# RWKV chunk pipeline: chunks seven phases apart instead of six, state-space groups every three steps instead of two

## The chip, the cores and the metric

The program runs on one core of one Trainium2 chip. The metric is the device time in microseconds (us) of one execution of the whole program. The core has a matrix engine (TensorE, PE in the rows; PEld is its weight load), a vector engine (VectorE, DVE), a scalar engine (ScalarE, ACT), GpSimd (POOL) and SyncE (SP), which only issues transfers here. Each engine works through its own list of instructions in order, and they wait for each other by semaphores.

## What is computed

Two layers of a decoder for a prompt of 2048 tokens and eight sample tokens. Layer 0 has an RWKV-7 recurrence and an S5 state-space layer side by side; the change touches only how these two are interleaved.

```
def step(s, inp):                      # RWKV-7, 8 heads of 64, for each token
    r_t, w_t, k_t, v_t, a_t, b_t = inp
    sa = jnp.einsum('bhvk,bhk->bhv', s, a_t)
    s = s * w_t[:, :, None, :] + sa[..., None] * b_t[:, :, None, :] + v_t[..., None] * k_t[:, :, None, :]
    return s, jnp.einsum('bhvk,bhk->bhv', s, r_t)
...
cr, ci, sr, si = lax.associative_scan(_cplx_combine, (a_re, a_im, bu_re, bu_im), axis=1)   # S5, 32 groups
h_re = sr + cr * h0r - ci * h0i
h_im = si + cr * h0i + ci * h0r
y = jnp.einsum('btgp,gcp->btgc', h_re, c_re) - jnp.einsum('btgp,gcp->btgc', h_im, c_im)
y = jax.nn.gelu(y)
```

## The kernel before

The program is a row of stages: projections of layer 0, the stage `rc` (function `rwkv_chunks`), the samples of layer 0, its output projection, then layer 1. Stages do not overlap: each ends with a barrier of all engines.

**RWKV.** In `rc` the 2048 tokens are 32 chunks of 64. The work of a chunk is 16 **phases** (`PHASES`), numbered 0 to 15 here. In each phase PE multiplies something into the chunk's own PSUM tile `bk` and then one other engine carries it to SBUF, for the next phase to read:

- phase 0 (`M_`): PE lines 1648 and 1651; DVE lines 1807, 1809, 1813. POOL then makes the masked tiles `ct` (line 1847)
- phase 1 (`KV`): PE 1660, 1664; ACT line 1763 (1024 columns)
- phases 2, 4, 6, 8, 10: PE 1726 to 1738; ACT line 1789 (512 to 1024 columns)
- phases 3, 5, 7, 9, 11: PE 1747 or 1749; DVE line 1833
- phase 12 (`SOLVE`): PE 1671; ACT 1767
- phase 13 (`LINK`): PE 1679; DVE 1816 and 1819
- phase 14 (`STATE`): PE 1691 to 1697; DVE 1828. This is the only phase that needs the chunk before, through the state `st`
- phase 15 (`OUT_`): PE 1704 to 1710; ACT 1773, after which ACT issues the stores of this chunk's output, two for an even chunk (line 1779) and four for an odd one (line 1783)

Time in the program is counted in **steps** t. In step t chunk c does phase t - LAG x c, if that is 0 to 15. With LAG 6 there are 202 steps (6 x 31 + 16), and two or three chunks are in flight: step 6n + r holds phases r, r + 6 and r + 12. Every engine's list is written step by step, in a step the oldest chunk first, and after the chunks of a step come the instructions of the state-space layer for that step (`s5.tensor`, `s5.vector`, and so on). Three buffers of each kind (`FLIGHT`) are used in turn.

**State space (class `StateSpace`, names `rc_s_`).** It has two sorts of work, pinned to steps:

- tables: DVE computes powers, cosines and sines. One piece, mostly two instructions of 512 columns, is done at the end of each step from step 6 on (`tables`, some 95 pieces), and 27 more pieces (`again`) between the two halves of the groups. In steps 52 to 68 PE also transposes the tables (lines 1338 to 1340), and ACT copies and stores each result (line 1296); the transposes of a step wait for the copy of the step before's
- 32 **groups**, of which g starts at step `at(g)`: PE does the products x (line 1348) in step at - 1; DVE the rotation and the scan (lines 1512 to 1518) in step at; DVE the lines 1526 to 1528 in step at + 1; PE the products y (lines 1362 to 1364), which read these, in step at + 2; ACT the GELU (line 1305) and its store in step at + 3. Before the change at(g) = 104 + 2g for the first 16 groups and 166 + 2(g - 16) for the others

So the stage has these stretches in steps: tables 6 to 104 (with the transposes at 52 to 68), groups 104 to 136, tables 136 to 166, groups 166 to 199.

Of the kernel before, what the change touches and what calls it, by code (L numbers as in the profile page):

```python
# [30 lines left out]
NCH = SEQ // CH  # L31
# [782 lines left out]
def project_even(nc, xT, w, z, z_last, mu_low, prm, w2, a2, const, ops, wc, bonus, sample_vecs):  # L814
# [7 lines left out]
    with Stage(nc, "pe") as s:  # L822
# [4 lines left out]
        def tile(count, width=WD):  # L827
            at, place[0] = place[0], place[0] + count * width
            t = work[:, at:at + count * width]
            return t.rearrange("p (n c) -> p n c", n=count) if count > 1 else t  # L830
# [336 lines left out]
G, SP_, GC = 32, 64, 16  # L1167
T8 = 8
NC8 = SEQ // T8
HG = G // 2  # L1170
# [4 lines left out]
class StateSpace:  # L1175
# [4 lines left out]

    BEGIN, LT, FIRST = 6, 52, (104, 166)
    MAPS = 8

    def __init__(self, s, u, par, mats, skip, const, y, fin, kept, trans, lags, bx, by):
# [25 lines left out]
            two("bi_st"), two("bi_in"), two("tq_in"), two("xt_in", 4), two("y_st"))  # L1212

    def at(self, g):
        return self.FIRST[g // HG] + 2 * (g % HG)

    def group(self, t):
        return next((g for g in range(G) if self.at(g) == t), None)
# [25 lines left out]
    def sync(self, sp, c):  # L1244
        if c == 1:
            for dst, src in ((self.pt[:, :, :], self.par), (self.raw[:, :, :, :], self.mats[:, 0:2]),
                             (self.m1[:, :, :], self.mats[:, 2]), (self.m2[:, :, :], self.mats[:, 3]),
                             (self.sg[:, :], self.const["sgn"]), (self.dd[:, :], self.skip),
                             (self.idt[:, :], self.const["ident"]), (self.jm[:, :], self.const["jm"])):
                sp.dma_start(dst, src).then_inc(self.cst, 16)  # L1250
            sp.dma_start(self.lags[0:7 * GC], self.const["zero_rows"]).then_inc(self.zeros, 16)
        if c == self.LT // 6 + 1:
            sp.wait_ge(self.L_ok, 1)
            for dst, src in ((self.kept[0], self.L[:, :, 0, :]), (self.kept[1], self.m1[:, :, :]),
                             (self.kept[2], self.sc[:, 8:10, :])):
                sp.dma_start(dst, src).then_inc(self.kst, 16)
        if c == self.LT // 6 + 5:
            sp.wait_ge(self.ks_ok, 1)
            sp.dma_start(self.lags[7 * GC:15 * GC], self.dd[:, :]).then_inc(self.kd, 16)
            sp.wait_ge(self.zeros, 16)  # L1260
            sp.wait_ge(self.kd, 16)
            for q in (0, 1):
                self.load_lags(sp, q)
        for g in range(G):
            if max(self.at(g) // 6, self.LT // 6 + 6) == c:
                self.load_x(sp, g)

    def sync_end(self, sp):
        for g in range(G):
            if self.at(g) // 6 >= NCH:  # L1270
                self.load_x(sp, g)
        sp.wait_ge(self.fout, 1)
        sp.dma_start(self.fin, self.fo[:, 3, :]).then_inc(self.kst, 16)
        sp.wait_ge(self.kst, 64)
# [220 lines left out]
    def vector(self, dve, t):  # L1495
        if t < self.BEGIN:
            return
        for late, step in ((self.first, self.FIRST[0]), (self.second, self.FIRST[1])):
            if t < step:
                if t < self.FIRST[0] or t >= self.FIRST[0] + G:  # L1500
                    next(late, None)
                break
            if t == step:
                for _ in late:
                    pass
        co, si, gs, xr = self.co, self.si, self.gs, self.xr
        g = self.group(t)
        if g is not None:
            e = g % HG
            dve.wait_ge(self.x_pe, g + 1)  # L1510
            dve.wait_ge(self.scan, g)
            dve.tensor_tensor(xr[:, 0, :], self.bx[:, 0:NC8], co[:, e, :], ALU.mult)
            dve.tensor_tensor(xr[:, 1, :], self.bx[:, NC8:2 * NC8], si[:, e, :], ALU.mult).then_inc(self.rot, 1)
            dve.wait_ge(self.rot, g + 1)
            dve.tensor_tensor(xr[:, 0, :], xr[:, 0, :], xr[:, 1, :], ALU.add).then_inc(self.summed, 1)
            dve.wait_ge(self.summed, g + 1)
            dve.wait_ge(self.hc_ok, g)
            dve.tensor_tensor_scan(gs[:, :], self.sc[:, 20, g:g + 1].broadcast_to([P, NC8]), xr[:, 0, :], 0.0, ALU.mult,
                                   ALU.add).then_inc(self.scan, 1)
        g = self.group(t - 1)  # L1520
        if g is not None:
            e, q = g % HG, g % 2
            dve.wait_ge(self.scan, g + 1)
            if g >= 2:
                dve.wait_ge(self.y_pe, g - 1)
            dve.tensor_tensor(self.hc[q][:, 1:NC8], gs[:, 0:NC8 - 1], co[:, e, 0:NC8 - 1], ALU.mult)
            dve.tensor_tensor(self.hs[q][:, 1:NC8], gs[:, 0:NC8 - 1], si[:, e, 0:NC8 - 1], ALU.mult)
            dve.tensor_copy(self.gl[:, g:g + 1], gs[:, NC8 - 1:NC8]).then_inc(self.hc_ok, 1)
            if e == HG - 1:
                half = slice(g + 1 - HG, g + 1)  # L1530
                dve.wait_ge(self.hc_ok, g + 1)
                dve.tensor_tensor(self.fo[:, 0, half], self.gl[:, half], co[:, :, NC8 - 1], ALU.mult).then_inc(self.flast, 1)
                dve.tensor_tensor(self.fo[:, 1, half], self.gl[:, half], si[:, :, NC8 - 1], ALU.mult).then_inc(self.flast, 1)
# [7 lines left out]
LEVELS = 5  # L1541
PHASES = 6 + 2 * LEVELS
(M_, KV, U0) = range(3)
FLIGHT, LAG = 3, 6
SOLVE, LINK, STATE, OUT_ = range(PHASES - 4, PHASES)
LV_W, LV_u, LV_U, LV_A, LV_B = range(5)

# [1 line left out]
def rwkv_chunks(nc, ops, wc, const, y, s_out, space):  # L1549
# [7 lines left out]
    with Stage(nc, "rc") as s_:  # L1557
# [79 lines left out]
        def _(pe):  # L1637
            def phase(c, ph):
# [74 lines left out]
                elif ph % 2 == 0:  # L1713
# [20 lines left out]
                    for g, r, s in tiles:  # L1734
                        pe.matmul(b[half[s], r, col(at, g)], ct[q][half[r], n, 2 * s + g, :], xx[q][half[r], s, g, :],
                                  start=True, stop=True)
# [246 lines left out]
def project_odd(nc, xT, w, z, cache_k, cache_v, table, bias, const, q_rows, cat):  # L1983
# [7 lines left out]
    with Stage(nc, "po") as s:  # L1991
# [82 lines left out]
        def _(pe):  # L2074
# [25 lines left out]
            for t in range(TAIL):  # L2100
                if pj.banks <= t < pj.slots:
                    pj.multiply(pe, t)
                if t == Q_AT:
                    pe.wait_ge(cst, 64)
                    pe.wait_ge(set_, 4)
                    pe.wait_ge(pj.evicted, pj.at[3, NBLK - 1] + 1)
                    for n in range(4):
                        mm = pe.transpose(stat[0:NS, n * P:(n + 1) * P], qc[:, n, :], idt[:, :])
                    mm.then_inc(q_tr, 1)
                if t - 2 in chain:  # L2110
                    later(chain[t - 2])
                for g in at(groups, t):
                    values(g)
                if t - PER - 4 in chain:
                    heads(chain[t - PER - 4])
# [1040 lines left out]
```

## Time and profile before

| | us |
|---|---|
| median of 3 runs | 3435.6 (3430.29 to 3436.28) |
| span of the profiled execution | 3435.7 |
| the stage `rc`, first to last matmul | 676.3 to 1296.8 |
| PE busy in the span | 2925.4 (85%) |
| DVE busy in the span | 2208.9 (64%) |
| ACT / POOL busy in the span | 1236.1 (36%) / 880.0 (26%) |

The profiled execution's span is used for sums; it lies 0.1 us from the median. Busy shares are means over stages with different limits, so the stage `rc` has to be read by itself, and within it each stretch: which engine works almost without a gap there, and for whom the others wait. In rows of the timeline, a start and a duration come first, and in brackets the idle time of the engine before it with the releaser.

### The profile page before, as it was taken

To read this page: it belongs to the slowest core of one execution; us is meant where nothing else is said; L and a number is where in the kernel's file an instruction comes from. 1 tells how busy PE (TensorE), PEld (TensorE's weight loads), DVE (VectorE), ACT (ScalarE), POOL (GpSimd) and SP (SyncE) were. 2 spreads that over 40 slices of the span, in tenths; PEclk is the share of its full clock that TensorE was granted. 3 is DMA by queue.
4 is the path that set the end of the run, shared out by engine and by line. 5 is a ranking of instruction groups with operands and counts; after the bars stand their busy time and mean duration, and the time that the engine had idled before them with its cause. 6 is when DMAs were issued, how large, how long until landed. Compare 5 with 4: busy or idle time off the path is not lost. (4 is left out here: it accounts for less than half of the span.)

```text
span 3435.7 us, 77289 instructions
## 1 busy us (share of the span) xinstructions
PE 2925.4 (85%) x31187; PEld 2453.0 (71%) x31187; DVE 2208.9 (64%) x3314; ACT 1236.1 (36%) x2205; POOL 880.0 (26%) x742
## 2 busy tenths in 40 slices
PE   8799999876779791899779999997986898996698
PEld 7699999766667670587679777875765666676576
DVE  3435666476676764687527777632437998895587
ACT  1015555333333330434201010111216888884432
POOL 4100000033233320211121111102114776763221
PEclk9899999888899995899889999998997999998899
DMA  4425455433334334655346999976432101007542
GB/s 161 164 88 149 145 153 154 135 82 87 92 90 114 77 99 114 185 164 157 136 148 208 332 344 329 348 244 193 151 123 100 47 17 63 14 2 193 193 147 87
DMA packets 486316, 500.80 MB, mean 146 GB/s; under 512 B 214273, under 2 KB 381426, under 8 KB 480954
## 3 DMA queue, kind: packets, MB, share of 16 engines
q1 hardware_dynamic: 371162, 332.49, 32.5%
q10 hardware_dynamic: 112752, 159.17, 13.7%
q0 software_dynamic: 2048, 4.20, 0.5%
q8 instruction: 249, 4.08, 0.5%
q14 instruction: 105, 0.86, 0.1%
HBM read 357.55 MB, written 138.41 MB: 144 GB/s over the span
## 5 line engine op out<-in xcount | busy, mean ns | idle before, releaser
L2494 POOL TENSOR_TENSOR sp_att<-sp_beta,sp_left 128x512 f32<-128x512 f32 (+3 forms) x320 | 318.4, 1006 | 195.8 <-DVE sp_left L2450 184.1
L1847 POOL TENSOR_TENSOR rc_ct<-rc_m,rc_lev 128x256 f32<-128x256 f32 x160 | 144.8, 926 | 825.4 <-DVE rc_m L1809 825.4
L102 PE MATMUL po_acc<-po_x_high,po_w_low 128*128 128x412 f32 (+1 forms) x840 | 306.8, 365 | 33.4 <-POOL po_w_low L95 15.2
L102 PE MATMUL pe_acc<-pe_x_high,pe_w_low 128*128 128x412 f32 (+1 forms) x840 | 305.0, 363 | 22.3 <-DVE pe_x_low L95 15.0
L103 PE MATMUL po_acc<-po_x_low,po_w_high 128*128 128x412 f32 (+1 forms) x840 | 299.4, 356 | 0.0
L104 PE MATMUL po_acc<-po_x_high,po_w_high 128*128 128x412 f32 (+1 forms) x840 | 299.1, 356 | 0.0
L104 PE MATMUL pe_acc<-pe_x_high,pe_w_high 128*128 128x412 f32 (+1 forms) x840 | 296.0, 352 | 0.0
L103 PE MATMUL pe_acc<-pe_x_low,pe_w_high 128*128 128x412 f32 (+1 forms) x840 | 295.6, 352 | 0.0
L2450 DVE TENSOR_TENSOR_SCAN sp_left<-sp_z,sp_left,sp_zero 128x512 f32<-128x512 f32 x192 | 235.3, 1266 | 14.1 <-ACT sp_z L2394 12.3
L2181 DVE TENSOR_TENSOR po_work<-po_work,po_q 128x1024 f32<-128x1024 f32 x128 | 174.7, 1365 | 84.4 <-DMA po_work<-in_cache_k 79.1
L102 PEld LDWEIGHTS po_acc<-po_x_high,po_w_low 128*128 128x128 f32 x840 | 162.8, 194 | 81.8 <-ACT po_o L801 30.7
L2386 ACT ACTIVATE sp_beta<-sp_z,sp_bias 128x512 f32<-128x512 f32 (+3 forms) x320 | 183.7, 632 | 71.4 <-PE sp_z L2325 43.7
L801 ACT COPY po_o<-po_acc 128x412 f32<-128x412 f32 (+1 forms) x105 | 52.5, 500 | 394.3 <-PE po_acc L104 372.2
L102 PEld LDWEIGHTS pe_acc<-pe_x_high,pe_w_low 128*128 128x128 f32 x840 | 159.8, 190 | 36.6 <-issue 24.3
L2394 ACT ACTIVATE sp_z<-sp_z,sp_bias_neg 128x512 f32<-128x512 f32 (+3 forms) x320 | 180.0, 615 | 0.0
L1789 ACT COPY rc_lv<-rc_bk 128x512 f32<-128x512 f32 (+2 forms) x160 | 112.8, 715 | 183.0 <-PE rc_bk L1738 157.3
L2340 PE MATMUL sp_t<-sp_id,sp_att 128*128 128x128 f32 x1088 | 154.3, 280 | 24.1 <-ACT sp_aT L2400 19.7
L2340 PEld LDWEIGHTS sp_t<-sp_id,sp_att 128*128 128x128 f32 x1088 | 117.4, 142 | 67.5 <-issue 64.9
L103 PEld LDWEIGHTS po_acc<-po_x_low,po_w_high 128*128 128x128 f32 x840 | 162.7, 194 | 1.0
L2355 PE MATMUL sp_ob<-sp_aT,sp_v 128*64 128x128 f32 x2176 | 155.3, 281 | 9.0 <-DVE sp_g L2464 9.0
L104 PEld LDWEIGHTS po_acc<-po_x_high,po_w_high 128*128 128x128 f32 x840 | 162.3, 193 | 0.7
L103 PEld LDWEIGHTS pe_acc<-pe_x_low,pe_w_high 128*128 128x128 f32 x840 | 159.7, 190 | 1.6
(450 smaller groups left out, 7323.7 us busy)
## 6 DMA issues: line engine op xcount, KB each, us to landing
po_work<-in_cache_k SPq DMA_DIRECT2D x256, 256.0 KB, 4.9
po_work<-in_cache_v ACTq DMA_DIRECT2D x256, 256.0 KB, 4.7
scratch_ops<-pe_work SPq DMA_DIRECT2D x160, 128.0 KB, 2.2
out_z<-pe_o SPq DMA_DIRECT2D x84, 206.0 KB
out_z<-po_o ACTq DMA_DIRECT2D x84, 206.0 KB
pe_w<-in_w_e SPq DMA_DIRECT2D x21, 512.0 KB
po_w<-in_w_o ACTq DMA_DIRECT2D x21, 512.0 KB
rc_opx<-scratch_ops SPq DMA_DIRECT2D x16, 640.0 KB
```

Of the source, the lines that this page charges most:

```text
L102: pe.matmul(out, ll, rh, start=start, stop=False)
L103: pe.matmul(out, lh, rl, start=False, stop=False)
L104: return pe.matmul(out, lh, rh, start=False, stop=stop)
L1789: act.copy(lv[q][:, :, lo:lo + count].rearrange("p s k g c -> p s (k g c)"), b[:, :, 0:count * 2 * CH]).then_inc(u_sb[n], 1)
L1847: pool.tensor_tensor(ct[q][:, n].rearrange("p (s g) c -> p s g c", s=2), m4[q][:, :, :, 0, :], spread(lev[:, n + 1, :]), ALU.mult).then_in ...
L2181: dve.tensor_tensor(kp[:, p % KR], kp[:, p % KR], qb[:, b % 2:b % 2 + 1, :].broadcast_to([P, 2, CW]), ALU.mult).then_inc(prod, 1)
L2340: mm = pe.transpose(tb[h][:, b * P:(b + 1) * P], att[h][:, n % 3, b * P:(b + 1) * P], idt[:, :])
L2355: mm = pe.matmul(ob[tile(n) % 2][c, 0:P], vt[m % 2][:, 4 * g + b, c], aT[h][:, n % 2, b * P:(b + 1) * P], start=(diagonal(n) and b == 0), ...
L2386: act.activation(be[h][:, n % 4, 0:w], zb[h][n % 2][:, 0:w], ACT.Sigmoid, scale=DC ** -0.5, bias=bt[:, head:head + 1]).then_inc(sig[h], 1)
L2394: act.activation(zb[h][n % 2][:, 0:w], zb[h][n % 2][:, 0:w], ACT.Sigmoid, scale=-DC ** -0.5, bias=nbt[:, head:head + 1]).then_inc(kept[h], 1)
L2450: dve.tensor_tensor_scan(row[:, at:at + w][:, ::-1], zb[h][n % 2][:, 0:w][:, ::-1], zero.broadcast_to([P, w]), start, ALU.mult, ALU.add).t ...
L2494: pool.tensor_tensor(att[h][:, n % 3, 0:w], be[h][:, n % 4, 0:w], left[h][tile(n) % 2][:, at + 1:at + 1 + w], ALU.mult).then_inc(at_ok[h], 1)
```

## The change

Chunks follow each other 7 steps apart (`LAG` 7), so the stage has 233 steps (7 x 31 + 16), and step 7n + r holds phases r, r + 7 and r + 14. A state-space group starts every third step (`STRIDE` 3), at steps 104 + 3g and 182 + 3(g - 16). The tables keep their pace of one piece a step and their place (6 to 104; the second lot is at 152 to 182), and the groups lie at 104 to 152 and 182 to 230. The step at which SP issues the transfers of a group follows from the same numbers. No instruction of the computation is added or removed.

```
-    BEGIN, LT, FIRST = 6, 52, (104, 166)
+    BEGIN, LT, FIRST, STRIDE = 6, 52, (104, 182), 3
...
     def at(self, g):
-        return self.FIRST[g // HG] + 2 * (g % HG)
+        return self.FIRST[g // HG] + self.STRIDE * (g % HG)
...
-        if c == self.LT // 6 + 1:
+        if c == self.LT // LAG + 1:
...
-        if c == self.LT // 6 + 5:
+        if c == self.LT // LAG + 5:
...
-            if max(self.at(g) // 6, self.LT // 6 + 6) == c:
+            if max(self.at(g) // LAG, self.LT // LAG + 6) == c:
...
-            if self.at(g) // 6 >= NCH:
+            if self.at(g) // LAG >= NCH:
...
-                if t < self.FIRST[0] or t >= self.FIRST[0] + G:
+                if t < self.FIRST[0] or t >= self.FIRST[0] + self.STRIDE * HG:
...
-FLIGHT, LAG = 3, 6
+FLIGHT, LAG = 3, 7
```

**VectorE in a stretch of tables.** Lines 1378, 1430 and 1434 are table work, the others carry phases. Before, from phase 11 of one chunk to phase 13:

```order
L1833 TENSOR_TENSOR rc_lv<-rc_lv,rc_bk 128x2x128
L1833 TENSOR_TENSOR rc_xx<-rc_xx,rc_bk 128x256
L1378 TENSOR_TENSOR rc_s_tmp<-rc_s_D,rc_s_sc 128x512
L1378 TENSOR_TENSOR rc_s_D<-rc_s_tmp 128x32x16
L1807 TENSOR_TENSOR rc_xx<-rc_bk,rc_lev 128x256
L1809 TENSOR_TENSOR rc_m<-rc_bk,rc_mask 128x512
L1813 TENSOR_TENSOR rc_xx<-rc_xx,rc_id 128x256
L1430 TENSOR_TENSOR rc_s_tmp<-rc_s_D,rc_s_sc 128x512
L1378 TENSOR_TENSOR rc_s_tmp<-rc_s_D,rc_s_sc 128x512
L1816 TENSOR_TENSOR rc_mt<-rc_bk,rc_id 128x256
L1819 TENSOR_TENSOR rc_rpt<-rc_bk,rc_ax 128x256
L1833 TENSOR_TENSOR rc_xx<-rc_xx,rc_bk 128x256
```

And now, over the same phases:

```order
L1833 TENSOR_TENSOR rc_lv<-rc_lv,rc_bk 128x2x128
L1378 TENSOR_TENSOR rc_s_D<-rc_s_tmp 128x32x16
L1434 TENSOR_TENSOR rc_s_tmp<-rc_s_D,rc_s_sc 128x512
L1833 TENSOR_TENSOR rc_xx<-rc_xx,rc_bk 128x256
L1378 TENSOR_TENSOR rc_s_tmp<-rc_s_D,rc_s_sc 128x512
L1378 TENSOR_TENSOR rc_s_D<-rc_s_tmp 128x32x16
L1816 TENSOR_TENSOR rc_mt<-rc_bk,rc_id 128x256
L1819 TENSOR_TENSOR rc_rpt<-rc_bk,rc_ax 128x256
```

Phases that VectorE carries now lie in nearly every step, one at a time with a piece of table after each; before, they came in pairs in every second step.

**TensorE in a stretch of groups**, from the end of one group's products y to the next y. Before (phases 11, 5, then x, phases 12, 6, 0, then y), two steps:

```order
L1749 MATMUL rc_bk<-rc_lv 64x64 x8
L1747 MATMUL rc_bk<-rc_lv 64x64 x8
L1348 MATMUL rc_s_x<-rc_s_xT,rc_s_bi 128x256 x2
L1671 MATMUL rc_bk<-rc_lv 64x128 x8
L1735 MATMUL rc_bk<-rc_xx,rc_ct 64x64 x8
L1738 MATMUL rc_bk<-rc_id,rc_xx 64x64 x8
L1648 MATMUL rc_bk<-rc_opx 64x128 x8
L1651 MATMUL rc_bk<-rc_opx 64x64 x8
L1362 MATMUL rc_s_y<-rc_s_xT,rc_s_tp 128x256
```

Now (phases 10, 3, 11, 4, 12, 5, then x and y), three steps:

```order
L1735 MATMUL rc_bk<-rc_xx,rc_ct 64x64 x8
L1738 MATMUL rc_bk<-rc_id,rc_xx 64x64 x8
L1747 MATMUL rc_bk<-rc_lv 64x64 x8
L1749 MATMUL rc_bk<-rc_lv 64x64 x8
L1726 MATMUL rc_bk<-rc_kt 64x64 x8
L1735 MATMUL rc_bk<-rc_xx,rc_ct 64x64 x8
L1738 MATMUL rc_bk<-rc_id,rc_xx 64x64 x8
L1671 MATMUL rc_bk<-rc_lv 64x128 x8
L1747 MATMUL rc_bk<-rc_lv 64x64 x8
L1348 MATMUL rc_s_x<-rc_s_xT,rc_s_bi 128x256 x2
L1362 MATMUL rc_s_y<-rc_s_xT,rc_s_tp 128x256
```

The products x and y of neighbouring groups stand in the same step now, directly behind each other; before, they stood in different steps.

**ScalarE after phase 15 of an odd chunk.** Before (the store's issue, a GELU, then the copies of phases 10 and 4):

```order
L1773 COPY rc_yb<-rc_bk 128x256
L1783 DMA scratch_y_a<-rc_yb 128x1x64 x4
L1305 ACTIVATE rc_s_yo<-rc_s_y 128x256
L1307 DMA scratch_y_b<-rc_s_yo 8x16x256
L1789 COPY rc_lv<-rc_bk 128x2x256
L1789 COPY rc_lv<-rc_bk 128x2x384
```

Now (behind the store stand the copies of phases 8 and 1 of the same step, then that of phase 2):

```order
L1773 COPY rc_yb<-rc_bk 128x256
L1783 DMA scratch_y_a<-rc_yb 128x1x64 x4
L1789 COPY rc_lv<-rc_bk 128x2x256
L1763 COPY rc_kt<-rc_bk 128x1024
L1789 COPY rc_lv<-rc_bk 128x2x512
```

Three copies for which TensorE waits stand directly behind the store's issue now.

## Rows read from the trace of the kernel before

**Rows 1.** The page: the span and how many instructions it holds.

```profile
span 3435.7 us, 77289 instructions
```

**Rows 2.** By stretch: us; busy us of PE, PEld, DVE, ACT, POOL; clock, DMA, GB/s

```profile
708.40:826.00 117.60, 83.16 (x3489) 75.99 (x3481) 94.26 (x164) 38.05 (x57) 45.16 (x42) 0.88 0.30 62
826.00:898.20 72.20, 52.22 (x1479) 49.46 (x1476) 39.77 (x80) 22.21 (x36) 15.99 (x16) 0.86 0.36 100
898.20:1003.30 105.10, 74.75 (x3078) 66.61 (x3078) 76.61 (x167) 33.17 (x49) 35.16 (x36) 0.92 0.36 85
1003.30:1105.00 101.70, 93.81 (x2935) 77.95 (x2934) 67.92 (x167) 34.85 (x59) 34.19 (x49) 1.00 0.48 122
1105.00:1194.30 89.30, 64.20 (x2570) 56.42 (x2570) 69.03 (x135) 27.59 (x42) 30.73 (x32) 0.92 0.30 66
1194.30:1296.80 102.50, 93.88 (x2751) 76.88 (x2750) 66.65 (x170) 31.77 (x57) 24.65 (x38) 1.00 0.40 100
```

**Rows 3.** Table transposes, then products x: ns min/median/max, first and last start.

```profile
L1338 PE MATMUL rc_s_x<-rc_s_id,rc_s_cos x32: 306/328/476, 829.4 to 897.6; 128*128 128x128 f32 x32
...
L1348 PE MATMUL rc_s_x<-rc_s_xT,rc_s_bi x128: 379/379/483, 1002.2 to 1285.7; 128*128 128x256 f32 x128
```

**Rows 4.** Timeline of VectorE in tables, one chunk: start, us, instruction, [idle before].

```profile
759.52 0.42 DVE L1833 TENSOR_TENSOR rc_lv<-rc_lv,rc_bk 128x256 f32<-128x256 f32 x1 [2.40 <-PE rc_bk L1749]
...
763.99 1.22 DVE L1430 TENSOR_TENSOR rc_s_tmp<-rc_s_cos,rc_s_sc 128x512 f32<-128x512 f32 x1
765.13 1.20 DVE L1378 TENSOR_TENSOR rc_s_tmp<-rc_s_jl,rc_s_sc 128x512 f32<-128x512 f32 x1
766.37 0.42 DVE L1816 TENSOR_TENSOR rc_mt<-rc_bk,rc_id 128x256 f32<-128x256 f32 x1
...
776.34 0.42 DVE L1833 TENSOR_TENSOR rc_lv<-rc_lv,rc_bk 128x256 f32<-128x256 f32 x1 [0.67 <-PE rc_bk L1749]
```

**Rows 5.** Who waited for whom in stage `rc`: us, times, longest.

```profile
PE rc_s_x L1338 <- ACT rc_s_bi L1296: 18.3, 12, 3.6
```

**Rows 6.** Timeline of TensorE in groups: start, us, instruction.

```profile
1054.46 0.41 PE L1735 MATMUL rc_bk<-rc_xx,rc_ct 64*64 64x64 f32 x16
...
1054.92 0.62 PE L1648 MATMUL rc_bk<-rc_opx 64*64 64x128 f32 x16
...
1055.70 0.70 PE L1362 MATMUL rc_s_y<-rc_s_xT,rc_s_tp 128*128 128x256 f32 x2
...
1057.19 0.68 PE L1679 MATMUL rc_bk<-rc_m,rc_hg 64*64 64x64 f32 x16
...
1058.07 0.27 PE L1747 MATMUL rc_bk<-rc_lv 64*64 64x64 f32 x2
...
1059.52 1.13 PE L1348 MATMUL rc_s_x<-rc_s_xT,rc_s_bi 128*128 128x256 f32 x4
...
1060.58 0.34 PE L1691 MATMUL rc_bk<-rc_hg,rc_lv 64*64 64x64 f32 x8
```

**Rows 7.** Groups of instructions, 1003.3 to 1105.0: busy us, mean ns, idle before.

```profile
L1518 DVE TENSOR_TENSOR_SCAN rc_s_gs<-rc_s_sc,rc_s_xr 128x256 f32<-128x256 f32 x16 | 11.9, 742 | 0.6
...
L1789 ACT COPY rc_lv<-rc_bk 128x512 f32<-128x512 f32 x16 | 9.4, 588 | 14.8 <-PE rc_bk L1738 9.3 <-issue 3.3 <-ACT rc_s_yo L1305 2.1
...
L1515 DVE TENSOR_TENSOR rc_s_xr<-rc_s_xr 128x256 f32<-128x256 f32 x16 | 9.2, 573 | 0.6
...
L1512 DVE TENSOR_TENSOR rc_s_xr<-rc_s_x,rc_s_cos 128x256 f32<-128x256 f32 x16 | 6.6, 413 | 0.0
...
L1763 ACT COPY rc_kt<-rc_bk 128x1024 f32<-128x1024 f32 x6 | 6.1, 1012 | 22.9 <-PE rc_bk L1664 22.9
...
L1809 DVE TENSOR_TENSOR rc_m<-rc_bk,rc_mask 128x512 f32<-128x512 f32 x5 | 3.4, 679 | 0.0
```

**Rows 8.** Timeline of ScalarE's queue: issue of an output store, even and odd chunk.

```profile
753.81 1.21 ACTq L1779 DMA_DIRECT2D scratch_y_a<-rc_yb  x2
...
772.23 2.69 ACTq L1783 DMA_DIRECT2D scratch_y_a<-rc_yb  x4
```

## The prediction

> **What bounds the kernel now.** The span is 3435.7 us [rows 1], 0.1 us above the median of the runs, so the sum goes straight against the median. Only the stage of the recurrence is touched, 676 to 1297 us. I read it by stretches [rows 2], whose borders come from the first and last transposes of the tables (steps 52 to 67) and products x (steps 103 to 195) [rows 3], and by the number of steps in each:
>
> - tables, steps 12 to 52: 117.6 us / 40 = 2.94 us a step. VectorE is busy 94.3 us (80%), TensorE 71%
> - transposes, steps 52 to 68: 72.2 / 16 = 4.51 a step, nothing over 72% busy
> - tables, steps 68 to 104: 105.1 / 36 = 2.92, VectorE 73%, TensorE 71%
> - groups, steps 104 to 136: 101.7 / 32 = 3.18, TensorE 92%, granted clock 1.00
> - tables, steps 136 to 166: 89.3 / 30 = 2.98, VectorE 77%, TensorE 72%
> - groups and end, steps 166 to 202: 102.5 us, TensorE 92%
>
> What is to be seen: two kinds of stretches with different limits. Where tables are made, the list of VectorE sets the pace. The timeline of one chunk there [rows 4] shows it going without a gap from a piece of table (two of 1.2 us, slower than elsewhere since POOL works at the same time) straight to phase 13, and TensorE waiting for that; its own waits there are 0.67 us at phase 11 and, for the chunk before, 2.40. Where groups run, TensorE goes almost without a gap and the others wait.
>
> So the 31 added steps are no time by themselves. The question is what a step costs in each kind of stretch.
>
> **Stretches of tables: the same number of steps, each lighter.** One piece of table a step stays. What thins out is the chunks' share. VectorE's work for a chunk is phase 0 (0.42 + 0.68 + 0.42), five times 0.42 for line 1833, 0.83 for phase 13 and 0.41 for phase 14 ([rows 4, 7] have 0.42 for 256 columns, 0.68 for 512): 4.85 us. In steps 12 to 52 VectorE is busy 2.36 us a step, of which 4.85 / 6 = 0.81 is chunks and 1.55 tables; 0.58 of each step is idle. With LAG 7 it is 1.55 + 0.69 = 2.24 busy.
>
> How much idle stays? I followed one chunk through seven steps by the rows' durations, from the end of phase 14 on VectorE. Odd phases (VectorE) and even ones (ScalarE) now share a step, so that while VectorE works on a table, the other half of the loop (TensorE, ScalarE, TensorE) gets done, and VectorE finds its next phase ready: it waits only about 0.4 us for phase 3 and 0.3 us before phases 0 and 14 each. The store behind phase 15 (2.7 us of ScalarE's queue for an odd chunk, 1.2 for an even one [rows 8]) lies in the one step in which VectorE has no phase, under two pieces of table in a row. That gives 16.8 us for seven steps; 0.5 more for a lower clock and TensorE's own pauses gives 17.3, or 2.47 a step. Savings against now: 40 x 0.47 = 19 us in steps 12 to 52, 36 x (2.92 - 2.50) = 15 in steps 68 to 104, 30 x (2.98 - 2.53) = 13.5 in the second lot. If VectorE had no gap at all, it would be 2.24 a step and 112 x 0.65 or so = 70 us in all; if the loop, not VectorE, set the pace, a step would stay at 2.9 and the saving nothing. I take 47.5: the one end is against the gaps that are there now [rows 4], the other against VectorE's 80%.
>
> **Transposes.** Here the loop goes in one line: chunk phases on TensorE, their copies on ScalarE, ScalarE's copy 1296, TensorE's next transposes, which wait for it [rows 5]. Seven steps carry the same phases as six did, and one more pair of transpose and copy: 28.4 us by addition against 25.6 for six, 4.06 against 4.27 a step. 16 x 0.2 = 4 us saved, with 0 to 8 as its bounds.
>
> **Stretches of groups: half as many steps again.** 32 groups times three steps are 96 steps, where there were 65. Bounds first. TensorE: with LAG 6 a chunk's phases and three groups fill 19.1 us (6 x 3.18). A group is y 1.49 us (1055.70 to 1057.19) and x 1.06 (1059.52 to 1060.58) [rows 6]; so a chunk is 19.1 - 7.7 = 11.4, of which about 1.4 are pauses: 10.0. Three steps of the new order are 3/7 x 10.0 + 2.55 = 6.85 us of work without a gap, 7.15 with the pauses. That would be the price if TensorE stayed the limit.
>
> But the new order closes a loop. The y of a group stands in the last of its three steps, behind all phases and the next x; the first phases of the next step stand behind y; VectorE's phase needs those, its scan stands behind its phase, then the next step's phase, then lines 1526 to 1528, and only then the next y. Over three steps, from the end of one y to the end of the next: phases on TensorE (blocks: phase 6 0.46, 0 0.78, 13 0.88, 7 0.28, 1 1.17 [rows 6]; the others by their number of matmuls), VectorE's phase, rotation and scan together 2.0 to 2.4 (0.41 + 0.41 + 0.57 + 0.74, more beside POOL), its next phase, TensorE's phases of the third step, x 1.06, y 1.49. With LAG 7 and three steps a group, seven cases take turns. Worked out in turn, for first steps with r = 3:
>
> y ends at 0; phases 10 and 3 done 0.78; VectorE's phase 3 to 1.25; scan to 3.35; phase 11 on VectorE (long ready) to 3.75; TensorE's 12 waited for it, 12 and 5 done 4.55; x 5.6; y 7.1 us.
>
> And for r = 0, the worst: phases 14, 7, 0 done 1.83; masks of phase 0 on VectorE to 3.3, scan to 5.7. Meanwhile phase 15 done 2.6, its copy 3.0, the store's issue until 5.7 for an odd chunk or 4.3 for an even one, copies of phases 8 and 1 (0.59 and 1.01 [rows 7]) to 7.3 or 5.9; phase 2 needs the latter, done 8.45 or 7.05; x, y: 11.0 or 9.6. On average 10.3.
>
> The seven, r = 0 to 6: 10.3, 9.8, 7.9, 7.1, 7.75, 8.5, 9.25; mean 8.66. This is against 6.3 for two steps now. TensorE would be 79% busy in it. In the stretches where it is 71% busy, the granted clock is 0.88 to 0.92, not 1.00 [rows 2], so I add 0.25 us for some slow matmuls and pauses: 8.9. The sum: 32 x 8.9 = 285 us, and 4.8 for the last three steps (as now), against 204.2 us now (101.7 + 102.5). That is +85.5 us. Bounds: 7.15 a group (+29) and 9.8 (+114).
>
> The Trainium skill ("TensorE: Matmul & The Clock Gate", "Loop structure matters more than you think") says that the order of the loops decides whether matmuls stay at the fast clock, and that waits between them lose it. By that rule the groups' stretches would fall to the clock of the tables' stretches, and with some 4 us of matmuls on the path, 10% of it makes 9.06 a group, 290 us; with the clock held it would be 8.66, 277 us.
>
> **Sum.** -47.5 - 4 + 85.5 = +34: 3470 us, slower by 1.0%. The point from which it turns is (204.2 - 4.8 + 51.5) / 32 = 7.84 us a group.
>
> **Rivals.**
>
> 1. TensorE stays the limit in the groups (faster). The loop hides better than I added up, since ready phases could stand ahead of the waiting ones more often. For it: TensorE goes 92% busy now, and 6.85 us of work is not far below 8.66. Against it: VectorE alone needs 5.2 us of each cycle (3/7 of 4.85, 2.1 for the scan, 1 for the three short lines 1526 to 1528), and part of it in a row with x and y. At 7.15 it is 3435.7 - 51.5 + 29 + 1 = 3414 us; at 7.6, 3428.
> 2. Steps with tables don't get shorter (much slower). The loop through ScalarE, not VectorE's list, would set 2.9 us a step. For it: VectorE also waits for TensorE now, once for 2.40 us [rows 4]. Against: its 80%, and the rows' durations, by which the loop is shorter than the list. Then 3435.7 + 85.5 = 3521 us; with half of the saving, 3495.
> 3. Both effects meet near the turning point, 7.6 to 8.1 us a group: 3429 to 3443 us.
> 4. SP falls behind with the groups' transfers, which would only add. I give it no chance of its own: they wait for the y of four groups before, which is ten steps ahead now and was six.
>
> **Chances.** The forecast 0.60, rival 1 0.22, rival 2 0.08, rival 3 0.10 (most of it within the bound of no change). Within 0.2% is about what a measurement of this kernel can tell from no change. Faster by over 0.2%: 0.25; within 0.2%: 0.10; slower by over 0.2%: 0.65. The range goes from 3418 us (part of rival 1) to 3505 (9.8 us a group, or half of rival 2).
>
> **What would show it.** Right: in the stretches of tables a step of about 2.5 us with VectorE over 88% busy; in the groups about 8.9 us from scan to scan (20.8 us a chunk), TensorE under 82% busy with a clock under 1.00, waits of TensorE for line 1833 and 1789 that were not there; line 1789 waiting behind the store's issue; the stage some 655 us long where it was 620. Wrong: scans 7.2 us apart with TensorE at 90%, or steps of 2.9 us in the tables. The rest of the program must not move.

## The result, and the profile after

The changed kernel takes 3473.8 us (median of 4 runs, 3472.5 to 3484.7); in the same session the kernel before took 3432.9 us (4 runs, 3428.4 to 3436.3). The ratio is 1.0126 with an interval of 1.0108 to 1.0143: slower by 1.3%. The forecast was 3470 us, slower by 1.0%.

The profiled execution spans 3473.0 us, against 3435.7 in [rows 1]. From the page: the span, and the busy time and number of instructions of each engine.

```profile
span 3473.0 us, 77286 instructions
...
PE 2922.3 (84%) x31187; PEld 2453.0 (71%) x31187; DVE 2204.6 (63%) x3314; ACT 1233.8 (36%) x2205; POOL 874.2 (25%) x742
```

TensorE has the same 31187 matmuls and is busy 2922.3 us, 3 us less than before. The longer span is time in which it waits. The stage `rc` runs from 675.1 to 1332.9 us, 657.8 us against 620.4, and the rest of the program is as long as it was (2815.2 and 2815.3 us).

The stretches are cut by the same rows as in [rows 3], here the first and last start of the tables' transposes (line 1338) and of the products x (line 1348):

```profile
L1338 PE MATMUL rc_s_x<-rc_s_id,rc_s_cos x32: 306/328/476, 814.2 to 877.4; 128*128 128x128 f32 x32
...
L1348 PE MATMUL rc_s_x<-rc_s_xT,rc_s_bi x128: 379/379/793, 966.0 to 1321.7; 128*128 128x256 f32 x128
```

The windows of these stretches, columns as in [rows 2] (window, us, then busy us and count of PE, PEld, DVE, ACT, POOL, granted clock, DMA share, GB/s):

```profile
706.80:812.10 105.30, 70.99 (x2972) 64.47 (x2969) 88.20 (x154) 30.55 (x46) 34.71 (x33) 0.89 0.30 61
812.10:878.50 66.40, 46.89 (x1311) 43.87 (x1305) 31.44 (x72) 20.73 (x34) 13.37 (x16) 0.89 0.39 109
878.50:967.10 88.60, 61.64 (x2599) 54.63 (x2598) 70.78 (x156) 28.26 (x42) 28.86 (x31) 0.94 0.39 91
967.10:1112.40 145.30, 114.31 (x3711) 98.24 (x3710) 80.93 (x190) 43.17 (x71) 41.75 (x57) 0.96 0.38 94
1112.40:1186.10 73.70, 52.80 (x2149) 46.87 (x2148) 61.21 (x121) 23.11 (x35) 24.87 (x25) 0.91 0.35 75
1186.10:1333.00 146.90, 115.85 (x3583) 98.66 (x3582) 77.23 (x188) 39.91 (x69) 35.59 (x51) 0.94 0.31 76
```

Beside [rows 2], with the forecast difference:

| stretch | steps | before us | after us | difference | forecast |
|---|---|---|---|---|---|
| tables, 12 to 52 | 40 | 117.6 | 105.3 | -12.3 | -19 |
| transposes, 52 to 68 | 16 | 72.2 | 66.4 | -5.8 | -4 |
| tables, 68 to 104 | 36 | 105.1 | 88.6 | -16.5 | -15 |
| second tables | 30 | 89.3 | 73.7 | -15.6 | -13.5 |
| 32 groups and the last 3 steps | 68, now 99 | 204.2 | 292.2 | +88.0 | +85.5 |
| sum | | | | +37.8 | +34 |

The second tables are steps 136 to 166 before and 152 to 182 after. So both halves of the forecast are there. A step with tables costs less once it carries less of a chunk, and a group, now of three steps, costs more than the tables give back. The spans differ by 37.3 us.

The waits in the groups' first stretch are of another size and kind. Who waited for whom (us, times, longest):

```profile
ACT rc_lv L1789 <- PE rc_bk L1738: 48.2, 23, 4.0
DVE rc_xx L1833 <- PE rc_bk L1747: 37.9, 14, 6.0
ACT rc_lv L1789 <- issue: 18.4, 7, 3.9
...
PE rc_bk L1747 <- ACT rc_lv L1789: 13.0, 12, 3.6
```

The same view of the kernel before, 1003.3 to 1105.0 us:

```profile
ACT rc_lv L1789 <- PE rc_bk L1738: 13.5, 13, 2.1
DVE rc_xx L1833 <- PE rc_bk L1747: 12.3, 6, 3.1
```

Before, ScalarE and VectorE waited for a TensorE that was 92% busy. Now TensorE itself is idle for 31.0 us (145.30 - 114.31), where it was 7.9. In the same view 21.9 us of this end with a copy by ScalarE (13.0 of them in the row above, the rest behind lines 1789 and 1767), 5.8 with VectorE. And line 1789 stands behind "issue" for 18.4 us (3.3 in [rows 7]). The timelines of one step show where that comes from. ScalarE's queue in the step that holds phases 15, 8 and 1 (r = 1) of an odd chunk, the step behind a product y:

```profile
1057.38 0.37 ACT L1773 COPY rc_yb<-rc_bk 128x256 f32<-128x256 f32 x1 [5.40 <-PE rc_bk L1710]
1057.78 3.81 ACTq L1783 DMA_DIRECT2D scratch_y_a<-rc_yb  x4
1061.64 0.58 ACT L1789 COPY rc_lv<-rc_bk 128x512 f32<-128x512 f32 x1 [3.88 <-issue]
```

TensorE and VectorE at the same time:

```profile
1062.28 0.46 PE L1747 MATMUL rc_bk<-rc_lv 64*64 64x64 f32 x16 [3.59 <-ACT rc_lv L1789]
```

```profile
1062.81 0.42 DVE L1833 TENSOR_TENSOR rc_xx<-rc_xx,rc_bk 128x256 f32<-128x256 f32 x1 [5.02 <-PE rc_bk L1747]
1063.14 0.42 DVE L1526 TENSOR_TENSOR rc_s_hc<-rc_s_gs,rc_s_cos 128x255 f32<-128x255 f32 x1
```

One store's issue (3.8 us for four DMAs) holds up TensorE and VectorE. Phase 8's copy (line 1789) stands behind it, TensorE's next phase waits 3.59 us for that copy, VectorE's phase 5.02 us for TensorE. Behind it come phase 1's copy, phase 2, x and the next y, which ends at 1069.3, 12.9 us after the one before. That is the path by which the prediction had its two longest cases, r = 0 and 1. Lines 1526 to 1528, which the next y needs, stand behind VectorE's phase, but they are done at 1065.0 and y starts at 1067.8, so it doesn't wait for them here.

### The profile page after: what moved, and what is told of

The parts are those of the page before. It is cut to its first block and busy times, and to the rows that moved or that the text cites. A ratio compares the mean times of both kernels' runs of the same rounds, so it can differ in the third digit from the quotient of the medians.

```text
span 3473.0 us, 77286 instructions
## 1 busy us (share of the span) xinstructions
PE 2922.3 (84%) x31187; PEld 2453.0 (71%) x31187; DVE 2204.6 (63%) x3314; ACT 1233.8 (36%) x2205; POOL 874.2 (25%) x742
## 5 line engine op out<-in xcount | busy, mean ns | idle before, releaser
L1847 POOL TENSOR_TENSOR rc_ct<-rc_m,rc_lev 128x256 f32<-128x256 f32 x160 | 135.7, 867 | 866.4 <-DVE rc_m L1809 866.4
L2340 PE MATMUL sp_t<-sp_id,sp_att 128*128 128x128 f32 x1088 | 154.4, 280 | 24.0 <-ACT sp_aT L2400 18.4
```

The lines of the kernel that those rows point to most:

```text
L1847: pool.tensor_tensor(ct[q][:, n].rearrange("p (s g) c -> p s g c", s=2), m4[q][:, :, :, 0, :], spread(lev[:, n + 1, :]), ALU.mult).then_in ...
L2340: mm = pe.transpose(tb[h][:, b * P:(b + 1) * P], att[h][:, n % 3, b * P:(b + 1) * P], idt[:, :])
```

## The experiments

All times are medians in us, and ratios are against the kernel before in the same session, with 95% intervals. Windows come from the one execution of each kernel that was profiled. A "group" below is the length of the two stretches of groups without the last three steps (4.8 us, or what is said), over 32; in the changed kernel it is (292.2 - 4.8) / 32 = 8.98, in the kernel before (204.2 - 4.8) / 32 = 6.23.

### One half alone: LAG 7, two steps a group

```
-    BEGIN, LT, FIRST, STRIDE = 6, 52, (104, 182), 3
+    BEGIN, LT, FIRST, STRIDE = 6, 52, (104, 166), 2
```

> Chunks seven steps apart as in the changed kernel, but a group every second step again (groups in steps 104 to 136 and 166 to 199, tables between). Loop theory (y, the next phases, scan, next phase, lines 1526 to 1528, next y is a closed loop over three steps, 9 us a group; over two steps TensorE is the limit again): 5.9 us a group, 189 us for 64 steps, then 34 steps of chunks alone at about 2.1 us, so about 3442 us, 30 under the changed kernel. Rival (it is the chunk distance, through ScalarE's store issue, that makes steps with groups slow): 6.6 us a group or more, 3465 us. Tables as in the changed kernel, 2.5 us a step, in both.

Measured: 3451.3 (6 runs), 1.0056 (1.0038 to 1.0075). Its windows of the two halves of the groups, and of the steps behind them that hold chunks alone:

```profile
972.20:1070.60 98.40, 88.30 (x2568) 72.11 (x2571) 69.80 (x162) 29.82 (x51) 29.02 (x42) 0.98 0.42 106
1145.50:1242.10 96.60, 89.77 (x2605) 73.35 (x2604) 70.41 (x167) 30.32 (x53) 31.09 (x44) 1.00 0.47 117
1242.10:1319.70 77.60, 53.66 (x2099) 47.71 (x2098) 18.45 (x45) 20.98 (x34) 14.56 (x18) 0.83 0.17 36
```

The total is 9 us over the 3442 expected. Groups of two steps take 6.1 us under LAG 7 ((98.4 + 96.6) / 32), as under LAG 6 (6.23), with TensorE 90% and 93% busy; 5.9 was expected, and the rival's 6.6 is out. The tables keep what they gained (-12.8, -15.9 and -14.4 us in the three stretches). But LAG 7 has 31 steps more, and behind the last group 34 steps are left in which only chunks run: 77.6 us, 2.28 a step, where the kernel before has 3. So LAG 7 by itself loses 21 us: the tables give 43, and an end without other work to hide in takes 73 (77.6 - 4.8). The forecast's 8.9 us a group belongs to the third step.

### The other half alone: LAG 6, three steps a group

```
-FLIGHT, LAG = 3, 7
+FLIGHT, LAG = 3, 6
...
-        STEPS = LAG * (NCH - 1) + PHASES
+        STEPS = max(LAG * (NCH - 1) + PHASES, s5.at(G - 1) + 4)
```

> The other half alone: chunks six steps apart, a group every third step (steps 104 to 152 and 182 to 230; 29 steps at the end have groups only). Loop theory: tables as before the change (2.9 us a step), groups about 9.2 us with chunks beside them and 4.8 us each for the last nine alone, so about 3482 us, nearly 50 slower than before the change. Rival (the chunk distance costs, the stride is free): groups at TensorE's 7.6 us, about 3445.

Measured: 3455.3 (5 runs), 1.0062 (1.0041 to 1.0084). The first half of the groups, then the end of the second half, where no chunk is left:

```profile
1004.70:1156.50 151.80, 125.73 (x4253) 108.38 (x4252) 83.86 (x202) 49.35 (x81) 47.00 (x65) 0.97 0.43 100
...
1295.40:1322.80 27.40, 23.23 (x97) 17.22 (x95) 25.01 (x69) 3.52 (x10) 2.36 (x8) 1.00 0.36 108
```

The first half takes 9.5 us a group (151.8 / 16), where 9.2 was expected; the rival's 7.6 is out. The total was expected at 3482 and came out 27 us lower, since groups without chunks cost 2.8 us each (27.4 us for their 29 steps) where I had 4.8, and in the second half groups with chunks cost 8.0. The two halves of the change each cost about 0.6%, and together 1.26%. That these numbers add up is chance: the loss of the first half alone sits in an end with chunks only, which the full change does not have.

### y in a step of its own

In the changed kernel y of one group and x of the next fall into the same step. Here y, and the GELU behind it (likewise from `t - 3` to `t - 4`), come a step later.

```
-        g = self.group(t - 2)
+        g = self.group(t - 3)
```

> The changed kernel with the products y of a group (and its GELU) one step later, so that they share the step with the next group's scan, as before the change, and no longer stand between lines 1526 to 1528 and the next phases. Loop theory: the loop opens, a group costs 7.3 to 7.6 us instead of 9.0, about 3425 us, which would beat both kernels. Rival (store issue on ScalarE or the number of steps sets the price): within 8 us of the changed kernel, 3466 to 3480.

Measured: 3451.9 (5 runs), 1.0055 (1.0036 to 1.0074). Transposes, then the two halves of the groups (the second with the end):

```profile
809.00:884.80 75.80, 56.58 (x1307) 53.37 (x1299) 31.91 (x72) 20.70 (x34) 13.06 (x16) 0.70 0.34 95
972.80:1107.90 135.10, 114.84 (x3703) 95.20 (x3702) 81.22 (x190) 42.58 (x70) 41.68 (x57) 0.97 0.42 99
...
1181.00:1318.30 137.30, 115.49 (x3583) 95.20 (x3582) 77.62 (x188) 40.40 (x69) 34.93 (x51) 0.96 0.33 82
```

The last three steps take 5.4 us here, as one more product y lies in them. A group falls from 8.98 to 8.34 us ((135.1 + 131.9) / 32), 20 us in all, but not to the 7.3 to 7.6 that a fully opened loop would have given. This alone can't say whether the gain comes from the opened loop or from taking y and x apart. The next two runs bear on that.

### x a step earlier

```
-        g = self.group(t + 1)
+        g = self.group(t + 2)
```

> The changed kernel with the products x of a group one step earlier, so that x and y no longer stand directly behind each other, while y stays where the change put it. Loop theory: x stands in the last piece of the cycle, before y, with 1.06 us; lines 1526 to 1528 are done a little before, so up to 1.0 us a group is given back: groups 8.0 to 8.4 us, 3445 to 3455 us. Rival (the loop closes over y and the scan alone, x lies in time that TensorE has to wait anyway): groups stay at 8.8 to 9.1, 3470 or more.

Measured: 3461.5 (9 runs), 1.0069 (1.0048 to 1.0091). Transposes and groups:

```profile
813.60:893.90 80.30, 61.20 (x1307) 57.91 (x1300) 31.49 (x73) 20.70 (x34) 12.61 (x15) 0.65 0.32 90
980.90:1120.40 139.50, 117.89 (x3708) 97.77 (x3708) 81.57 (x191) 43.49 (x71) 42.11 (x57) 0.95 0.40 97
1193.30:1322.00 128.70, 109.59 (x3454) 89.78 (x3454) 76.59 (x184) 39.75 (x68) 36.11 (x51) 0.99 0.35 86
```

(139.5 + 128.7) / 32 = 8.38 us a group, within the 8.0 to 8.4 expected, and the rival is out. y stays in the third step here, so the loop is as closed as before; only x has left that step. The gain is 19 us, the same as with y moved. What both share is that x and y (2.55 us of TensorE together, [rows 6]) no longer stand in one step ahead of the next phases. The total is over the 3445 to 3455 expected and by medians only 12 us under the changed kernel. The profiled execution lost 14 us in the transposes, at a clock of 0.65 (see the last section); whether the other eight did is not known.

### The reverse in the kernel before: x and y brought together

LAG 6 and two steps a group, with y and its GELU one step later, which there puts y into the step of an x:

```
-        g = self.group(t - 2)
+        g = self.group(t - 3)
```

> The kernel before the change with y one step later. Theory: with a group every second step TensorE is the limit in the groups (93% busy), so where y stands changes nothing: 6.3 us a group, 3428 to 3436 us. Rival (the loop through y also costs with two steps): a gain of 8 us or more, as it gave 22 in the changed kernel.

Measured: 3442.2 (10 runs), against 3432.4 (18 runs) before: 1.0026 (1.0010 to 1.0043), slower.

```profile
1005.30:1116.70 111.40, 95.26 (x2935) 81.16 (x2934) 68.20 (x172) 34.51 (x59) 34.41 (x49) 0.97 0.45 109
...
1203.60:1305.10 101.50, 88.88 (x2617) 75.05 (x2616) 64.20 (x166) 30.39 (x55) 25.33 (x38) 0.98 0.38 98
```

The groups take 212.9 us where they took 199.4 (204.2 - 4.8): 13.5 us lost. Neither of the two cases written down was right. The distance from scan to y grew by a step, and the time grew too. All of the loss is idle time of TensorE, 28.8 us in the two stretches where it was 15.1; in the first half it falls from 92% to 86% busy (95.26 / 111.40). The lump of x and y is one reading. Another was not tested: with y a step later the buffers that it reads come free a step later as well. POOL's copy of an operand for a later y (line 1323) waits 62.2 us for y in the first half, where it waited 32.2. The products x, before which TensorE never stood idle, have 8.0 us of idle time before them, 2.4 of it for the transfer of their table and 5.6 with no releaser in the profile; but the 8.8 us before y are gone. So this run agrees with the lump and doesn't show it.

### The store's issue behind everything of its step

The stores stay on ScalarE, but are issued after its copies of phases 8 and 1.

```
+                while late:
+                    store(late.pop(0))
```

> The changed kernel with the issue of a chunk's output store moved behind all other ScalarE work of its step, so that the copies of phases 8 and 1 no longer wait behind it. Loop theory: on the path in two of the seven cases (r = 0 and 1), 0.55 us a group, and little in the tables: 3450 to 3456 us. Rival (the store issue is the main cost): groups fall to 7.2 us, about 3419 us.

Measured: 3446.5 (9 runs), 1.0046 (1.0028 to 1.0065), a little under what was expected; the rival's 7.2 us a group is out. Tables of steps 12 to 52, transposes, groups:

```profile
706.70:801.60 94.90, 65.32 (x2972) 57.84 (x2968) 88.88 (x154) 31.26 (x46) 35.34 (x34) 0.99 0.30 64
801.60:878.60 77.00, 58.07 (x1316) 54.85 (x1306) 32.70 (x73) 20.89 (x34) 13.21 (x15) 0.69 0.36 97
964.00:1109.50 145.50, 118.38 (x3713) 101.14 (x3712) 78.37 (x190) 43.85 (x71) 40.63 (x57) 0.93 0.39 94
1185.30:1321.00 135.70, 108.24 (x3455) 92.23 (x3454) 73.90 (x184) 39.65 (x67) 35.10 (x51) 0.97 0.33 82
```

The first tables take 2.37 us a step, under the forecast 2.47, and VectorE is busy 94% of them. So the store's issue ahead of the copies was what kept that stretch at 2.63. In the groups moving it helps little (281.2 us for 287.4), since the issue now stands ahead of phase 2's copy in the next step. After an odd chunk's store:

```profile
1063.13 1.50 ACT L1794 COPY rc_lv<-rc_bk 128x1024 f32<-128x1024 f32 x2 [3.26 <-issue]
```

From the end of one y to the end of the next, the case r = 0 falls from 11.3 to 8.4 us (means of four), and the case r = 1, in which phase 3 waits for that copy, rises from 11.3 to 12.2.

### The stores issued by SP

SP issues the stores of a chunk three chunks later in its own list (`FLIGHT` is 3), so that it doesn't wait long for `y_sb`. The last groups' loads (`sync_late`) are taken out of `sync_end`, so that they stay ahead of the last stores. ScalarE issues none in this stage but its own tables' and groups'.

```
+                if c >= FLIGHT:
+                    store(c - FLIGHT)
+            s5.sync_late(sp)
+            for c in range(NCH - FLIGHT, NCH):
+                store(c)
...
-                    act.wait_ge(y_sb, c + 1)
-                    out = y[:, :, tokens(c)]
...
-                            act.dma_start(out[:, s::2], yb[0][:, 2 * s:2 * s + 2, :]).then_inc(y_st[0], 16)
```

In the changed kernel (LAG 7, three steps):

> The changed kernel with the output stores of a chunk issued by SyncE instead of ScalarE (three chunks later, where SyncE stands behind that chunk anyway), so that nothing stands between phase 15's copy and the copies of phases 8 and 1. Theory of two costs (the store's issue in front of phase 8's copy, and the closed loop through y): step r = 1 falls from 5 us to 2.5 to 3.5 in tables, 11 us saved in steps 12 to 52, 8 in the transposes, 18 to 20 in the groups (8.4 us a group): 3430 to 3440 us. Rival (loop only, store hidden as the prediction had it in the tables): 3452 to 3460, all of the gain in the groups.

Measured: 3443.1 (10 runs, 3436.3 to 3452.2), 1.0029 (1.0015 to 1.0043), 3 us over the expected range. Against the changed kernel the stage gets 41 us shorter in the profiled executions (617.1 for 657.8), of which this one was the fastest of its ten; by medians the difference is 31 us. ScalarE in a step with phases 15, 8 and 1, where it had the gap of 3.88 us (lines have moved by 8 to 18):

```profile
1031.75 0.37 ACT L1791 COPY rc_yb<-rc_bk 128x256 f32<-128x256 f32 x1 [5.40 <-PE rc_bk L1728]
1032.22 0.59 ACT L1797 COPY rc_lv<-rc_bk 128x512 f32<-128x512 f32 x1
```

First tables, transposes, and the groups (the second half with the end):

```profile
706.20:800.40 94.20, 65.45 (x2973) 57.71 (x2965) 88.89 (x154) 31.93 (x47) 37.22 (x34) 1.00 0.32 68
800.40:859.10 58.70, 41.35 (x1300) 38.70 (x1300) 32.90 (x73) 20.23 (x34) 12.98 (x15) 1.00 0.45 125
...
944.90:1080.10 135.20, 111.39 (x3711) 95.95 (x3710) 78.53 (x190) 43.88 (x71) 40.70 (x57) 0.99 0.42 100
...
1155.50:1291.90 136.40, 108.50 (x3583) 92.95 (x3582) 75.18 (x188) 40.44 (x69) 35.18 (x51) 1.00 0.33 82
```

With the stores on SP the first tables are 11.1 us shorter, the transposes 7.7 and the groups 20.6 (8.98 to 8.34); the other two stretches of tables moved by -2.8 and +1.7. Not all of this is waiting. TensorE's idle time falls by 5.6 us in the first tables (34.3 to 28.8) and by 10.3 in the groups (60.5 to 50.2). The rest is its own busy time, shorter at a granted clock of 1.00 where it was 0.89, and of 0.99 and 1.00 where it was 0.96 and 0.94. Whether the shorter waits brought the clock with them is not shown: the run with the store behind everything had 0.93 and 0.97 in its groups with TensorE 81% and 80% busy, this one 0.99 and 1.00 with 82% and 80%. The Trainium skill ("TensorE: Matmul & The Clock Gate", "Loop structure matters more than you think") gives a long DMA wait before every matmul as the case that goes cold. No wait of that kind is in these stretches: the longest wait of TensorE in them is 2.6 us, behind a copy, and the clock stayed at 0.99 and 1.00 with a fifth of the time idle.

The two things taken together, the stores on SP and y a step later:

> Changed kernel with both: stores on SyncE and y one step later. Theory of two costs, added: 22 us for the loop (as measured for y alone) and 35 to 40 for the store: 3412 to 3418 us, groups at 7.5 to 7.8 us. Rival (the same waits, counted twice): no better than the stores alone.

Measured: 3428.4 (10 runs), 0.9979 (0.9962 to 0.9997).

```profile
804.00:876.50 72.50, 55.38 (x1314) 52.13 (x1303) 32.79 (x73) 20.89 (x34) 12.79 (x15) 0.72 0.39 104
962.10:1087.00 124.90, 111.89 (x3706) 92.97 (x3705) 79.53 (x190) 43.18 (x70) 41.90 (x57) 1.00 0.43 105
1164.40:1290.40 126.00, 110.47 (x3449) 91.11 (x3448) 75.10 (x184) 39.97 (x67) 35.68 (x51) 0.96 0.35 88
```

7.84 us a group, just above the 7.5 to 7.8 expected; 36.5 us of the 59 between 8.98 and TensorE's 7.15 are thus accounted for, where the two effects apart make 20.6 and 20.4. TensorE is busy 6.95 us of a group and idle 0.89. In the first stretch about half of the idle time (6.7 of 13.0 us) ends with "issue", with no releaser in the profile, so what holds the last 0.7 us a group stays open. The total is 10 us over the 3412 to 3418 expected; the profiled execution, the slowest of its ten, took 14 us more in the transposes than the one of the run before (72.5 for 58.7).

The stores on SP with LAG 7 and two steps a group:

> Seven steps, a group every second step, stores on SyncE. Theory: groups at TensorE's limit (5.7 to 5.9 us), tables 2.37 us a step, the last 34 steps of chunks alone shrink from 2.28 to about 1.9 us each: 3408 to 3415 us. Rival (TensorE and VectorE are the limit and the store is hidden): 3440 or more.

Measured: 3428.8 (10 runs), 0.9977 (0.9958 to 0.9996). Groups, then the end with chunks alone:

```profile
947.30:1037.00 89.70, 86.55 (x2571) 71.07 (x2574) 66.38 (x162) 30.31 (x51) 29.58 (x43) 1.00 0.46 115
1114.30:1210.40 96.10, 90.98 (x2605) 74.51 (x2604) 67.02 (x167) 30.81 (x53) 30.58 (x44) 0.98 0.49 118
1210.40:1281.60 71.20, 50.21 (x2099) 43.60 (x2098) 18.44 (x45) 21.29 (x34) 14.67 (x19) 0.93 0.19 39
```

5.8 us a group as expected, but the end takes 2.09 us a step where I had 1.9. The total is 14 us over the 3408 to 3415 expected.

And the stores on SP in the kernel before (LAG 6, two steps):

> The kernel before the change with the same move of the stores to SyncE. Theory: with six steps the store's issue only delays the copies of phases 10 and 4, groups are limited by TensorE and don't move (6.3 us a group), tables and transposes gain 10 to 18 us: about 3418 us, which would beat both kernels. Rival (the store never costs with six steps): 3428 to 3433, no change.

Measured: 3413.2 (4 runs, 3409.0 to 3416.0) against 3433.0 (25 runs): 0.9932 (0.9909 to 0.9955). First tables, transposes, and the first half of the groups:

```profile
705.90:820.00 114.10, 79.10 (x3488) 71.18 (x3478) 95.57 (x164) 38.31 (x57) 44.97 (x42) 0.93 0.31 65
820.00:882.90 62.90, 47.77 (x1481) 45.10 (x1473) 39.64 (x80) 21.97 (x36) 15.92 (x16) 0.95 0.42 114
...
980.60:1083.80 103.20, 94.62 (x2935) 78.27 (x2934) 67.73 (x167) 35.31 (x60) 34.31 (x49) 1.00 0.46 116
```

The groups stay as they were (103.2 us for 101.7 in [rows 2]), since TensorE is 92% busy there and hides the issue. The tables gain 14 us (117.6 + 105.1 + 89.3 against 114.1 + 97.7 + 86.5) and the transposes 9, these at a higher clock. The total is 5 us under the expected 3418, since tables and transposes gave 23 us, not 10 to 18. This kernel beats both the kernel before and the changed one: 20 us under the first, 61 under the second.

## Why the prediction was right, point by point

- **The sum.** 3470 us forecast, 3473.8 measured. All five terms have the right sign, and the largest miss is 6.7 us, so the terms are not two large errors that cancel. That the total came within 4 us is luck in part: four runs of the changed kernel spread over 12 us, and the stretch of transposes alone differed by 14 us between kernels with the same instructions in it.
- **Tables.** "The list of VectorE sets the pace, so thinning the chunks' share shortens a step": 2.63, 2.46 and 2.46 us a step for the forecast 2.47, 2.50 and 2.53. The step that failed in the first stretch is "the store behind phase 15 lies ... under two pieces of table in a row". It doesn't. ScalarE's queue for an odd chunk there:

```profile
733.65 3.40 ACTq L1783 DMA_DIRECT2D scratch_y_a<-rc_yb  x4
737.10 0.58 ACT L1789 COPY rc_lv<-rc_bk 128x512 f32<-128x512 f32 x1 [3.48 <-issue]
...
738.26 0.42 DVE L1833 TENSOR_TENSOR rc_xx<-rc_xx,rc_bk 128x256 f32<-128x256 f32 x1 [2.19 <-PE rc_bk L1747]
```

  The copy of phase 8 comes 3.48 us late. The two pieces of table that were to hide this end 2.4 us after the issue begins (at 736.1), and VectorE then stands idle for 2.19 us. The step takes 6.9 us there for an odd chunk and 5.1 for an even one, counted on TensorE from the start of phase 15 to that of phase 9; the other six of a chunk are left with (7 x 2.63 - 6.0) / 6 = 2.07. With the issue out of the way of the copies the stretch fell to 2.37 and 2.36 (94.9 and 94.2 us / 40). I had also priced the issue from [rows 8] at 2.7 us, and it took 3.4 here. In the other two stretches of tables moving it to SP brought 2.8 and -1.7 us, so there the cover did hold. The bound "112 x 0.65 or so = 70 us" has a slip: the three stretches have 106 steps, and 0.70 us each makes 75. The sum doesn't use it.
- **VectorE over 88% busy in the tables** was wrong: 84%, 80% and 83%. In the first stretch by the store. In the others a step needs less of VectorE than I took: 70.78 / 36 = 1.97 and 61.21 / 30 = 2.04 us, not 2.24, which came from the first stretch.
- **Transposes**: -5.8 for -4, but that is no support. In the four kernels of this study with LAG 7 and the stores where they were, the same instructions took 66.4 to 80.3 us. The addition was also low by itself: it has 4.27 and 4.06 us a step, the traces 4.51 and 4.15.
- **Groups.** The seven cases of a group in order, from the end of one y to the end of the next, forecast and measured (means over the groups): r = 0: 10.3 and 11.3; 1: 9.8 and 11.25; 2: 7.9 and 8.64; 3: 7.1 and 6.4; 4: 7.75 and 7.83; 5: 8.5 and 8.1; 6: 9.25 and 9.28. Mean of the seven 8.66 (8.9 with the clock) and 8.97. The order is right but for r = 2, which came out above r = 5. The mis-sized ones are the two with a store in them, each 1 us or more short, and r = 2 behind them; r = 3 was 0.7 too long.
- **The clock.** 0.96 and 0.94, between the two cases that were weighed (the tables' level of 0.88 to 0.92, or held at 1.00). The groups took 287.4 us, against 290 and 277 by these cases.
- **The mechanism.** The prediction said that a loop closes through y: first phases, scan, the next VectorE phase, lines 1526 to 1528, "and only then the next y". Its last link isn't there. For y (line 1362) and what ended TensorE's idle time before it, the view has:

```profile
L1362 PE MATMUL rc_s_y<-rc_s_xT,rc_s_tp x64: 379/379/634, 974.8 to 1327.0; 128*128 128x256 f32 x64
...
  DVE rc_s_glast L1528: 0.6, 2
```

  Over all 32 groups y waited twice for these lines, 0.6 us in sum. The scan shows up one link earlier, as the walk for r = 3 had it: phase 12 (line 1671) waits for VectorE's phase 11 five times, 3.9 us in sum. The larger waits go through ScalarE's copies, 21.9 of 31.0 us in the first stretch of groups, as the walk for r = 0 had it. The runs show what was worth something. With x and y in different steps the groups got 19.2 us shorter (x moved) and 20.4 (y moved), with 19.8 and 19.1 us less idle time of TensorE; with the issue away from ScalarE they got 20.6 shorter, half of it idle time. A longer distance from scan to y did no more than moving x, and in the kernel before it went with a loss of 13.5 us. So the size was right and the walks were right where they follow the copies; the loop through lines 1526 to 1528 did not set it.
- **Rivals.** 1 is out: TensorE is 79% busy in the groups, and even with both causes removed a group takes 7.84 us, not 7.15. That is also just the forecast's turning point of 7.84, and the kernel there (3428.4) is 0.2% under the one before; it has the stores' gain in the tables too, and a slow stretch of transposes against it. 2 is out: steps with tables got shorter by 44 us in sum. 3 is out with 8.98 us a group. 4: no wait of TensorE for a transfer shows up in the groups.

## What to carry to other kernels

Where work of several kinds shares one sequence of steps, the number of steps says little about the time. Here the stretches of tables, whose steps kept their number and lost work, got shorter (2.9 to 2.5 us a step). The groups, which got half as many steps again with the same work, went from 6.23 to 8.98 us each, and the end with chunks alone cost 2.1 to 2.3 us a step. So count the cost stretch by stretch, and try a side job's large pieces on one engine (x and y) in different steps. And look at which engine issues the DMAs: four issues held ScalarE 2.7 to 3.8 us, in front of a copy for which TensorE waited, and moving them to SyncE's queue was worth 20 us to the one kernel and 31 to the other.

## What the runs showed of the hardware that I had not expected

- **The transposes' stretch has no fixed time.** With LAG 7 (about 1300 matmuls) it took 58.7 us at a granted clock of 1.00, 61.0 at 0.94, 66.4 at 0.89, 70.5 at 0.79, 72.5 at 0.72, 75.8 at 0.70, 77.0 at 0.69 and 80.3 at 0.65. Four of these eight kernels have the same instructions there and still differ by 14 us (66.4, 70.5, 75.8 and 80.3). Nearly all of it is the clock: TensorE's idle time in the stretch is 17.1 to 17.4 us in the three kernels with the stores on SP and 18.9 to 19.5 in the five others, while its busy time goes from 41.4 to 61.2. So the stores' issue was worth about 2 us of waiting there. What makes the clock differ stays open. The kernels with 9 or 10 runs spread over 16 to 28 us, the kernel before over 19 in 25 runs; whether this stretch makes that spread isn't shown, since only one run of each was profiled. For the small differences the stretches of groups were therefore compared, not totals; they too come from one execution each.
- **What an issue costs the issuing engine.** Four DMAs kept ScalarE's queue for 2.69 us in [rows 8], 3.40 and 3.81 us in the rows above: 0.67 to 0.95 us each, in a queue that also has to copy.
